# RWKV-7 scan: products, masks and the triangular inverse laid out anew, and another order of work on each engine

## What is computed

```python
def step(s, inp):
    r_t, w_t, k_t, v_t, kk_t, a_t = inp
    sa = jnp.einsum('bhvk,bhk->bhv', s, -kk_t)
    s = s * w_t[:, :, None, :] + sa[..., None] * (kk_t * a_t)[:, :, None, :] + v_t[..., None] * k_t[:, :, None, :]
    return s, jnp.einsum('bhvk,bhk->bhv', s, r_t)
```

## Time and profile before

| what | value |
|---|---|
| median of three runs | 2646.19 us |
| the profiled execution, its own time | 2639.5 us |
| its span, first to last instruction | 2637.5 us |
| mean granted TensorE clock | 0.959 |
| busy, share of the span: PE, PE weight loads, DVE, ACT, POOL | 88%, 65%, 38%, 31%, 12% |
| matmul records in all / on 64x64 quarters | 28347 / 20480 |
| the scan, from the first staged keys to the last state | about 1454 to 2041 us |

### The profile page before, as it was taken

The page is one execution under the profiler, slowest core; times in us unless marked ns, Lnnn a source line. Parts: engine busy times, 40 slices in busy tenths (PEclk is TensorE's granted clock), DMA queues, the critical chain, the costliest instruction groups (busy, mean ns, idle before and its releaser), DMA issues. The chain is left out here.

```text
span 2637.5 us, 62574 instructions
## 1 busy us (share of the span) xinstructions
PE 2315.8 (88%) x28347; PEld 1725.5 (65%) x28347; DVE 996.2 (38%) x1987; ACT 824.6 (31%) x1692; POOL 324.0 (12%) x478
## 2 busy tenths in 40 slices
PE   5999966879899999979997778787787789999999
PEld 3555434545688888865543667676676458888887
DVE  0000055651542244223115666666763144323421
ACT  3211145430321121120002676666674032112211
POOL 0000013110000000000000444445443000000000
PEclk8999989889999999999998899999999899999999
DMA  8223100741022222220110000000000302222221
GB/s 299 107 86 128 42 3 31 269 158 48 25 72 73 71 71 73 72 72 32 64 40 20 8 7 9 9 9 10 9 6 6 112 15 66 78 66 77 68 77 59
DMA packets 160757, 168.16 MB, mean 64 GB/s; under 512 B 13788, under 2 KB 117996, under 8 KB 160364
## 3 DMA queue, kind: packets, MB, share of 16 engines
q1 hardware_dynamic: 160492, 164.16, 19.5%
HBM read 160.61 MB, written 3.54 MB: 62 GB/s over the span
## 5 line engine op out<-in xcount | busy, mean ns | idle before, releaser
L170 PE MATMUL psum<-arena 64*64 64x64 f32 (+5 forms) x20480 | 1131.3, 259 | 217.4 <-issue 55.5
L170 PEld LDWEIGHTS psum<-arena 64*64 64x64 f32 (+3 forms) x20480 | 771.2, 145 | 573.2 <-issue 437.3
L170 PEld LDWEIGHTS psum<-arena,weights 128*128 128x128 f32 x2048 | 385.8, 188 | 89.7
L170 PE MATMUL psum<-arena,weights 128*128 128x128 f32 x2048 | 392.5, 273 | 0.0
L170 PE MATMUL psum<-norm_high,weights_high 128*128 128x512 f32 x512 | 246.0, 481 | 14.1 <-DVE norm_low L498 14.1
L170 PE MATMUL psum<-hidden_high,weights_high 128*128 128x512 f32 x512 | 244.0, 476 | 0.0
L551 ACT ACTIVATE weights_high<-weights 128x2048 fp32r<-128x2048 f32 x62 | 118.5, 1911 | 354.9 <-PE psum L170 354.9
L170 PE MATMUL psum<-norm_high,weights_low 128*128 128x512 f32 x512 | 203.6, 398 | 0.0
L170 PE MATMUL psum<-hidden_high,weights_low 128*128 128x512 f32 x512 | 202.2, 395 | 0.0
L170 PE MATMUL psum<-norm_low,weights_high 128*128 128x512 f32 x512 | 201.9, 394 | 0.0
L170 PE MATMUL psum<-hidden_low,weights_high 128*128 128x512 f32 x512 | 200.4, 392 | 0.0
(11 more groups left out here) (182 smaller groups left out, 2468.7 us busy)
## 6 DMA issues: line engine op xcount, KB each, us to landing
weights<-in_mlp_w SPq DMA_DIRECT2D x64, 1024.0 KB, 5.8
arena<-in_ada_w SPq DMA_DIRECT2D x24, 2048.0 KB, 9.6
arena<-in_ab_w_in SPq DMA_DIRECT2D x6, 2048.0 KB, 8.5
arena<-in_ab_w_out SPq DMA_DIRECT2D x2, 2048.0 KB, 8.8
arena<-in_rwkv_wr SPq DMA_DIRECT2D x2, 2048.0 KB, 10.5
arena<-in_rwkv_wk SPq DMA_DIRECT2D x2, 2048.0 KB, 8.2
arena<-in_rwkv_wv SPq DMA_DIRECT2D x2, 2048.0 KB, 7.9
arena<-in_rwkv_wo SPq DMA_DIRECT2D x2, 2048.0 KB, 10.9
```

What stands on the lines that cost most here:

```text
L170: return nc.tensor.matmul(out, lhsT, rhs, start=start, stop=stop, skip_group_check=shared)
```

## The change

- **Layout.** Keys `b` and `k` lie in `BKD` side by side, `b` first for d=0 and `k` first for d=1; values and corrections in one tile `UV` on different halves of the partitions. GR becomes one product of 64 rows and 128 columns of weights for both keys (8 products, 128 columns each, two banks), which DVE masks with two instructions. The readout products of B3 and the value products of the walk go. BT is eight transposes. s becomes 4 + 4 products a step over all 128 partitions. u is 8 products a step, x 4. The value part of x is computed ahead (XV), beside B2.
- **Inverse.** B3, B4, B5 are three times Y = D + N Y (8 products each), each added to D by DVE. One N is kept instead of two, ACT copies 256 columns of it and 256 of XV.
- **Engines.** DVE instead of ACT takes x out (it adds XV); ACT takes u out with two instructions instead of one; the bonus is scaled by ACT. POOL: s2 is one instruction over both directions instead of two; P1 is four half-partition instructions instead of one whole and two half; the "plus one" of B2 goes; values are staged each iteration with four half-partition copies instead of four a head pair.
- **Order.** All four lists are new.
- The masks C_DIAG and C_OFF are 320 columns shorter, and L1680 (k_raw) goes; its factor is folded into ACT's square and DVE's product.

By the calls an iteration has 184 products: 144 in the tasks and 40 in the walk. Of these 8 are transposes.

```diff
-        PE_ORDER = (("A3", 1), "BT", "B5", ("s1", -1), ("item2", -1), ("G", 2), ("B1", 1), "x0", "item0", ("A1", 2), "u0", ("B2", 1), ("GR", 1),
-                    "s0", ("A2", 2), "x1", ("B3", 1), "item1", "u1", ("B4", 1))
...
+        PE_ORDER = ("B4", "item0", ("G", 2), ("s1", -1), "B5", ("GR", 1), "x0", ("A1", 2), ("B1", 1), "u0", "item1", "s0", ("B2", 1), ("A2", 2),
+                    "x1", ("B3", 1), ("BT", 1), "u1", "item2", ("A3", 2))
+        DVE_ORDER = ("item0", ("G", 2), ("s1", -1), "B5", "keys0", "keys3", "y_sum", "x0", ("GR", 1), "staging0", "item1", "s0", "staging3",
+                     "y_norm0", "staging1", "keys1", "x1", "y_norm1", "staging2", ("B3", 1), ("bonus_raw", 1), "keys2", "cum0", "staging4", "item2",
+                     ("A3", 2), ("cum1", 1), ("B4", 1))
+        ACT_ORDER = (("u1", -1), "decays1", ("item2", -1), "decays3", "decays0", "item0", ("y1", -1), "decays4", "k_square", "u0", ("B1", 1),
+                     ("A1", 2), "item1", "decays2", ("B2", 1), ("A2", 2), ("BT", 1))
+        POOL_ORDER = (("A2", 1), ("x1", -1), ("G", 2), ("B0", 1), "x0", ("A1", 2))
...
+            def read_keys(m):
...
+                for hh, d, h, c in units_of(m):
+                    ins = mm(PS[:, 6 + h, 256 * d + 128 * hh:256 * d + 128 * hh + 128], BKD[d][HALF[h], c, :], ARD[d][HALF[h], c, :])
...
+                for hh, h, d in ALL8:
+                    c0 = 128 * h + 64 * hh
+                    last = mm(PS[HALF[d], 2, c0:c0 + 64], QO[m % 2][HALF[d], h, 0, hh, :], DD[HALF[d], h, 1, hh, :])
+                    c0 = 128 * step_of(d, hh) + 64 * h
+                    ins = mm(PS[HALF[d], 3, c0:c0 + 64], KB[m % 2][HALF[1 - d], h, d, hh, 0:64], UV[m % 2][HALF[1 - d], step_of(d, hh), 2 * d + h, :])
...
+            def second_block(m):
+                pe.wait_ge(S("b_vector"), 4 * m + B_VE["Y1"])
+                on_token(2, NT[:, :, 0], Y1[:, :, 0]).then_inc(S("b_product"), 1)
...
+                for hh, d, h, c in units_of(m):
+                    ins = nc.tensor.transpose(PS[:, 6 + h, 128 * d + 64 * hh:128 * d + 64 * hh + 64], BKD[d][HALF[h], c, :],
+                                              CON[HALF[h], C_ID + 64 * h:C_ID + 64 * h + 64])
...
             def walk_s(n, s):
                 k = 2 * n + s
                 pe.wait_ge(S("rwkv_u"), k + 1)
-                for d, hh, c, r, t in each_dh(n, s):
-                    mm(PS[r, 4 + d, 192 + 64 * hh:256 + 64 * hh], US[k % 2][t, d, :], BRM[n % 2][t, d, 0, hh, :],
+                for d, h, hh, c in each_dh(n, s):
+                    mm(PS[HALF[h], 4 + d, 192 + 64 * hh:256 + 64 * hh], UV[n % 2][:, s, 2 * d + h, :], KB[n % 2][:, h, d, hh, 64:128],
                        start=False, stop=True, shared=True)
...
+                for z, r in enumerate(HALF):
+                    ins = A.activation(UV[n % 2][r, s, 2 * z:2 * z + 2, :], PS[r, 4:6, 64:128], ACT.Copy)
+                ins.then_inc(S("rwkv_u"), 1)
...
+            def walk_x(n, s):
+                dve.wait_ge(S("rwkv_x_psum"), 2 * n + s + 1)
+                dve.wait_ge(S("b_scalar"), 4 * n + B_SC["XV"])
+                V.tensor_tensor(XS, PS[:, 4:6, 0:64], XV[n % 2][:, s], ALU.add).then_inc(S("rwkv_x"), 1)
...
-                step(G.tensor_tensor(P1[:, 0, 0], QD[:, 0, 0], units(slice(0, P)), ALU.add))
...
+                for d, r in enumerate(HALF):
+                    for h in range(2):
+                        ins = G.tensor_tensor(P1[HALF[h], d, 0], QD[r, h, 0], units(r), ALU.add)
+                        if (d, h) != (1, 1):
+                            step(ins)
...
+                for z in range(2):
+                    for part in range(2):
+                        d = 1 - z
+                        ins = G.tensor_copy(UV[m % 2][HALF[z], step_of(d, part), 2 * d:2 * d + 2, :],
+                                            RV[HALF[part], tile_of(i, d), 128 * q:128 * q + 128].rearrange("p (h v) -> p h v", h=2))
```

More of the change, by code:

```diff
@@ L57, in constants @@
     near = s // 16 == t // 16
[L58 to L61, removed]
+    up, down = np.where(i < 64, s < t, s > t), np.where(i < 64, s > t, s < t)
+    for b in range(4):
+        c[:, C_DIAG + 64 * b:C_DIAG + 64 * b + 64] = near & (up if b < 2 else down)
+    c[:, C_OFF:C_OFF + 64] = ~near & up
     c[:, C_I64:C_I64 + 64] = s == t
@@ L1155, in program, with take_at @@
         spans = [[U_H * T, (U_H + 8) * T], [(U_MID + 3) * T, ARENA]]
[L1157 removed]
+        def take_at(n):
             for span in spans:
@@ L1188, in program @@
         G2 = take(256).rearrange("p (s c) -> p s c", s=2)
[L1189 to L1195, removed]
+        pe_at = take_at(64)
+        PE_ = flat(pe_at, 40).rearrange("p (s d c) -> p s d c", s=2, d=2)
+        QD, A1, A2, DD = blocks4(2), blocks4(2), blocks4(3), blocks4(2)
+        QO, TTs = ([blocks4(), blocks4()] for _ in range(2))
+        P1, P3, IQ, IQ8, NT, Y1, Y2 = (blocks4() for _ in range(7))
+        KB = [take(1024).rearrange("p (h d w x) -> p h d w x", h=2, d=2, w=2) for _ in range(2)]
+        BTs = [take(512).rearrange("p (h d w x) -> p h d w x", h=2, d=2, w=2) for _ in range(2)]
         R, K = unit(U_R, 8), unit(U_RK, 8)
@@ L1652, in rwkv_act @@
             decays(0, 0)
-            tasks = dict(A1=squares, A2=fourths, B1=diagonal, B2=off_diagonal, B4=near_inverse, BT=turn_keys, B5=inverse_of,
-                         x=walk_x, u=walk_u, y=walk_y)
+            tasks = dict(A1=squares, A2=fourths, B1=diagonal, B2=off_diagonal, BT=turn_keys)
+            tasks.update(dict(u=walk_u, y=walk_y))
             aux = {"k_square": (0, 1, k_square), "decays0": (2, 1, decays, 0), "decays1": (3, 1, decays, 1),
@@ L1878, in rwkv_pool @@
             pool.wait_ge(S("rwkv_prompt_zero"), 1)
-            aux = {"values0": (3, 1, values, 0), "values1": (3, 1, values, 1)}
-            tasks = dict(G=start, A1=squares, A2=fourths, B2=off_diagonal, x=s2)
+            tasks = dict(G=start, A1=squares, A2=fourths, B0=values)
+            tasks.update(dict(x=s2))
             for n in range(-4, NB + 2):
-                run_iteration(n, POOL_ORDER, tasks, aux=aux)
+                run_iteration(n, POOL_ORDER, tasks)
         def rwkv_sp(sp):
```

291 lines of the change are left out of this document (136 added, 155 removed).

## The result

The changed kernel takes **2633.69 us** (median of 5 runs, 2632.86 to 2637.29), the kernel before on the same chip 2646.48 (5 runs, 2643.56 to 2653.37): ratio **0.9948**, 95% interval 0.9933 to 0.9963. It is faster, by 12.8 us where 60 were forecast, and 1.7 us outside the upper end of the range. The profiled execution took 2637.29 us, its span 2635.5.

What follows compares the result with a forecast made beforehand. Supply of TensorE's instructions was taken as the bound, with waits on top; 2.96 packets of 4.33 us make 12.8 us an iteration for 14.3, forty give 60 us off 2639.5, and with 6.7 added 2586 us; range 2540 to 2632.

Steps and rivals of the forecast that it cites:

- The supply: TensorE's instruction packets on queue 8 bound the scan; 3.65 an iteration fall to 2.96, and issue waits below 1 us.
- 0.55 W + F: Packet interval: W is TensorE's work and waits per packet, F = 2.3 us until new instructions run; 3.96 us becomes 4.33.
- TensorE's work: Sum of TensorE's task times an iteration, items included: 9.8 us before, 9.0 after, with 0.6 more for shape changes.
- the changes 0.6: TensorE going from quarters to other shapes and back four times an iteration (GR, BT, s0, s1), 0.15 us each.
- the full bound: Upper bound for one shape change there and back on TensorE: 0.22 us, four an iteration, 0.9 us.
- The waits: TensorE's waits for other engines an iteration: 1.2 us before, sum 1.6 after, rounded down to 1.4.
- the +0.3 for the two: GR's waits for var and the sigmoids: 0.45 us less cover in three iterations of five, +0.3 us.
- of which I count 0.3 net of what the supply hides: A3's wait for ACT's copy of A2 and POOL's step after it: +0.3 to +0.7 us an iteration, counted as 0.3.
- Rival B: DVE's turn-around bounds: 2.9 us idle kept beside 11.0 of work, 13.9 us an iteration, 2630 us; chance 0.18.
- Rival A: Packets keep their 3.96 us, so 2.96 of them make 11.7 us an iteration, 2542 us; chance 0.15.
- Rival C: POOL's eight half instructions in the diagonal blocks' chain decide from 1.03 us each; at 1.1 us, 2666 us; chance 0.10.
- Rival D: Fewer products, no time gained: supply waits become waits for ACT and DVE one for one, 2646 us; chance 0.05.

Runs made afterwards that it cites:

- Both edits of var: Var's banks given back behind the Ln, and one table load for Ln and Exp: 0.9954 in the kernel before, 0.9895 in the changed kernel.
- records brought back: Changed kernel with 40 products an iteration issued twice (16 in G, 16 in A1, 8 in B1): ratio 1.0195 to the kernel before.
- the eight edits to s, r's product, both, x (three), u and item1: Changed kernel; half of s's rows 0.9968, r's decay product out 0.9966, both 0.9935, x 0.9998, 1.0034, 1.0017, u 0.9983, item1 1.0124.
- One move: Changed kernel with item1 behind the state products in TensorE's and VectorE's lists, ScalarE's left as it was: 1.0124 of the kernel before.
- the filler: Eight 128 x 128 products, results unread, ahead of GR's wait for var's banks: 0.9947 in the changed kernel, 0.9896 (2616.11 us) with both var edits.

## Why the prediction was wrong in its size

**The supply: right, with its levels off.** Packets in 400 us fell from 101 to 84 (an iteration takes 2.9 instead of 3.6; forecast 2.96 and 3.65), the interval is 4.76 us (forecast 4.33), and "issue" is 0.1 us an iteration, under the 1 us named. But the formula, 0.55 W + F with F = 2.3, put 3.3 us of stalls into an iteration before and left 1.8 after it. By the rows there were 1.6, and 0.1 are left. The 1.5 of difference came out right, by two levels that were both too high; the earlier trace rows had the level, 41.7 us in 28 iterations, and the formula went past it. What the rows of before said plainly is that all the supply could give was 1.6 us an iteration, some 63 us, and the forecast was that gain in full.

**TensorE's work: the new tasks right, the sum mis-sized.** The sum of the tasks was to fall from 9.8 to 9.6 us an iteration. Busy time by the profile rose from 11.3 to 11.6. This term is off by about 0.4 us an iteration, 17 us of 47. The tasks that change their shape are not what it missed. Here are s1, GR, s0 and BT, from each one's first product to the next task's, with the columns of the earlier trace rows:

```profile
1616.59:1617.20 0.61, 0.61 (x22) 0.55 (x16) 0.48 (x1) 0.61 (x3) 0.00 (x0) 1.00 0.00 0
1617.81:1618.90 1.09, 1.09 (x20) 0.97 (x16) 0.91 (x4) 0.74 (x3) 0.93 (x3) 1.00 0.00 0
1622.28:1622.90 0.62, 0.62 (x20) 0.55 (x16) 0.00 (x0) 0.62 (x2) 0.25 (x1) 1.00 0.00 0
1624.80:1625.19 0.39, 0.39 (x12) 0.33 (x8) 0.27 (x1) 0.38 (x1) 0.00 (x0) 1.00 0.00 0
```

They take 2.71 us with their changes of shape, where the forecast had 2.65 (s 0.9, GR 0.85, BT 0.3, the changes 0.6). The run with half the rows of s agrees: it put s back on quarters and took 0.7 us off the busy time, as much as the forecast had for that. The end of a product ahead of a wait counts as busy, but that doesn't explain the rise either: TensorE waits 124 times in 500 us before and 103 times after. Part can be the stretches at the lower clock, 27 us in 500 for 14. The rest is open. The timeline shows one change of shape, the transposes of BT between two pieces on quarters:

```profile
1621.27 3.60 PE L170 MATMUL psum<-arena 64*64 64x512 f32 x128 [0.47 <-DVE arena L1749]
1624.81 0.46 PE L1499 MATMUL psum<-constants,arena 64*128 64x64 f32 x8
1625.20 0.73 PE L170 MATMUL psum<-arena 64*64 64x64 f32 x16
```

With a product's 0.22 to 0.24 us from start to end, the last quarter product starts at 1624.65, the first transpose 0.16 us later, the last transpose at 1625.03, and the quarters resume 0.17 us later: with normal steps of 0.05, 0.2 us for both, the full bound of the earlier trace rows. The Trainium skill, page "TensorEngine Tiling (Array Packing)", section Tiling Modes, says that a change of tiling mode drains the engine. The trace agrees in that a change costs 0.1 us more than a step; that the array is empty by then it does not show, since the next product starts 0.16 us after the last, whose length is 0.22 in the profile.

**The waits: the step that failed.** "Waits of PE, 1.2 before ... Sum 1.6 ... Rounded down ... 1.4." They are 2.2, from 1.3. var went from 0.5 to 0.7 us an iteration and the sigmoids (L1554) from 0.2 to nearly none, so that the +0.3 for the two did not come; the copy of x went as forecast. What was not counted, or netted away, are the many small ones: y's copy, G behind L1756, N's copy, item1 behind the masks, the blocks behind L1760, the A tasks behind GpSimd, the copy of u. With the last rows of the answer they come to 1.4 us an iteration where the like of them came to 0.3. Against the forecast the waits are off by 0.7 us an iteration, 28 us: with the term above about the missing 47. The step is one sentence of the prediction that has no row: "of which I count 0.3 net of what the supply hides". The stalls for instructions, 1.6 us an iteration, had been cover for answers of the other engines, by my reading; the forecast took them away and kept the cover. Three runs show such an exchange. Both edits of var in the kernel before take 0.4 us an iteration off the waits for engines, and 0.2 comes back as stalls for instructions; in the changed kernel, which has no such stalls, the same edits take 0.35 off and bring it in full. With records brought back the waits fall by 0.4 as stalls rise by 0.5, though there 1.4 us of work came with them, which is cover too. With work taken from s the waits rise by 0.6 for 0.7. No run takes the stalls away and leaves order and tasks as they were, so how the 0.9 us of new waits divide between the lost cover and the new lists stays open.

**Rival B** gave 13.9 us an iteration and 2630 us; 13.93 and 2633.7 were measured, and its mark, 2.9 us of VectorE's waits kept, is met with 2.8. The sum is right in part by luck: it was 11.0 of VectorE's work and these 2.9, and the runs show 10.3 of work, 2.8, and 0.8 of other waits. Its mechanism is met by half. An answer of VectorE behind x's wait costs half of its length, ahead of the wait a quarter, and to give x to ScalarE makes the kernel slower. It is not one engine's turn-around but a round in which the walk, the diagonal blocks and the banks of the items run through lists that were written to fit each other. That last sentence is argued from the eight edits to s, r's product, both, x (three), u and item1, which all moved the time less than, or against, their own length, and not shown by one.

**Rival A** (11.7 us) fell: waits filled what the packets left. **Rival C** fell as placed: the half instructions took 504 ns, under the 827 of the earlier trace rows and half of the 1.03 from which they decide. GpSimd did become slower elsewhere, L1871 850 ns for the 664 of L1851:

```profile
L1864 POOL TENSOR_TENSOR arena<-arena,constants 64x128 f32<-64x128 f32 x112 | 56.4, 504 | 100.2 <-DVE arena L1740 93.6
L1871 POOL TENSOR_TENSOR arena<-arena,constants 128x256 f32<-128x256 f32 x57 | 48.5, 850 | 122.2 <-ACT arena L1626 62.8 <-ACT arena L1630 59.4
```

The Trainium skill, page "GPSIMD Engine Reference", section Key points, names contention with VectorE's instructions that have two SBUF inputs or run in a 2-port mode. VectorE is at 74% for 67% here, but what it does more (the second mask of GR, the blocks, the addition to x) reads PSUM for one input, so it is not shown that this is the cause; the two lines also differ in what they add to, and no run here takes them apart. **Rival D**, stalls turned into waits one for one, had the mechanism nearest to what was found, and a chance of 0.05: the exchange is about two for three (waits 0.9 for 1.5, and busy 0.2 beside them).

VectorE's work is 10.3 us an iteration (74% of 13.93), 11.0 forecast; GpSimd's fell from 6.8 to 5.8 where about +1 was forecast, its new half instructions (504 ns) and copies (289 ns) being shorter than the rows that priced them.

What stays open: how much of the waits a new order of the tasks could take back. One move was tried, in two of the three lists that it touches, and cost 45 us.

## What to carry to other kernels

When a stall is taken away that was spread over the whole loop, ask which answers of other engines arrived during it: they were free, and can become waits. The gain has a ceiling that one row gives (idle time for that cause, per iteration), and a forecast at the ceiling needs a reason why nothing is late next. The wait that did count in full, in the kernel without stalls for instructions, was the longest single one (4.45 us, once a head pair), and it was cut by giving a bank back behind its last reader rather than behind the last instruction of the task: with one table load for two functions 16 us, more than the whole change brought. The fastest version measured is the changed kernel with these two edits, 2618.84 us, or 2616.11 with the filler, which can't be told from it.

## What the runs showed of the hardware

TensorE's busy time can rise, in the profile, when products are taken away: 17% fewer records and 4% more busy time in 400 us. A change between quarters and another shape took 0.15 us from product to product where a normal step is 0.05. Waits of 4.45 us without products, and of 2.40 us in the kernel with both edits of var, were followed by 3.4 to 6.8 us at the lower clock, in six of the head pairs; eight products of 128 columns in it and a shorter wait left none of these stretches, and gave some 5 us for 27 at the lower level. 64 small records an iteration cost 15 to 23 us in a kernel with 0.1 us of supply stalls and 25 to 28 us in one with 1.6; their busy time was 0.5 to 0.7 us of it an iteration.
